# Attention begun behind four of the eight key tiles, the other four projected between its first steps

## The chip, the core and the metric

The kernel runs on one core of a Trainium2 chip. Its engines work side by side, each through its own stream of instructions in order: TensorE (PE) for matmuls, with its weight loads shown as a lane of their own (PEld), VectorE (DVE), ScalarE (ACT), GpSimd (POOL) and SyncE (SP), which here issues the loads of weights. They are ordered among each other by semaphores alone. The metric is the time of one execution on the device in microseconds (us); less is better.

## What is computed

A trunk of two layers over 512 tokens of width 1024. Layer 0 is a recurrent mixer and an MLP; layer 1 is latent attention and an MLP. The change is in the attention of layer 1, eight heads, whose part of the reference is:

```python
q = (rmsnorm(c_q, q_norm) @ w_uq).reshape(B, T, MLA_HEADS, MLA_NOPE + MLA_ROPE)
kv = (rmsnorm(c_kv, kv_norm) @ w_ukv).reshape(B, T, MLA_HEADS, MLA_NOPE + MLA_V)
q_nope, q_rope = q[..., :MLA_NOPE], q[..., MLA_NOPE:]
k_nope, v = kv[..., :MLA_NOPE], kv[..., MLA_NOPE:]
q_rope = rope(q_rope, cos[:, :, None, :], sin[:, :, None, :])
k_rope = rope(k_rope, cos, sin)
# per block of 128 queries, with a block-causal mask over chunks of 64:
s = (einsum('bqhd,bkhd->bhqk', qn, k_nope) + einsum('bqhd,bkd->bhqk', qr, k_rope)) * scale
p = softmax(where(key_chunk <= q_chunk, s, -inf))
o = einsum('bhqk,bkhv->bqhv', p, v)
```

## The kernel before

**Split precision.** Every large product is made of three matmuls (`mm3`, line 1459): a value x is held as a rounded high part and the rest as a low part. So each result that feeds another product is read out of PSUM twice: ACT writes the high part (`key_high`, `query_high`, `rope_high`, `split_high` for weights), DVE subtracts and writes the low part (`key_low`, `query_low`, `rope_low`, `split_low`), and both count up semaphores (kt_high and kt_ready for keys, qn_high and qn_ready for queries, qr_high and qr_ready for rotated queries, hi_ready and lo_ready for weights).

**Units of weights.** Weights come in units, numbered in the order of their use: here ("mv", 0), ("mv", 1), ("qr", 0), ("qn", 0), ("mk", 0), ("mk", 1), then ("qr", a), ("qn", a) for a = 1 to 3, then the output projection. A unit is loaded into one of two stages; SP issues unit u only when unit u - 2 has been split by ACT and by DVE (`stage_free`, line 537 and on). It is then split into one of four slots. `pump(u)` on ACT and on DVE splits unit u + 4 into the slot of unit u; on ACT it first waits until the last tile that uses unit u is done (`tile_of_unit`).

**Tiles and two banks.** A projection is a tile of [128 features x 512 tokens], made by `feature_tile` (line 1469 and on). Tiles are numbered in the order of `add_tile`, tile n goes to bank n % 2, and `wait_bank` (line 455) makes PE wait, ahead of tile n, until tile n - 2 has been read: for a key tile "read" is kt_ready (its low part is written), for ("qn", ...) it is qn_ready, for ("qr", a) it is rot_read (DVE's `rotate(a)` is through). A key tile ("mk", g, j) of head 4g + j has 6 matmuls of 512 columns, a tile of ("qr", a) or ("qn", a, hh) has 9. ("qr", a) holds the rotary part of two heads: DVE multiplies it by cosine and sine (`rotate`), POOL issues four DMAs that swap its halves, DVE adds (`rotated`), ACT and DVE write high and low (`rope_high`, `rope_low`).

**Order around the change.** PE projects ("qr", 0), ("qn", 0, 0), ("qn", 0, 1) and all eight key tiles. Then comes a loop of steps j = 0 to 33, j = 4 h + qb for head h and block of queries qb. In step j PE makes scores(j) (two matmuls of k_rope, three of k_nope, one of the mask, all of width (qb + 1) x 128), then a tile where one is due: ("qr", a) in step 0 of a group of eight, ("qn", a, 0) in step 3, ("qn", a, 1) in step 5, for a = 1 to 3; then transposes(j - 2) of the probabilities; and in each step of j % 4 == 2, from 6 on, values(j // 4 - 1), the product of head j // 4 - 1 with its values. DVE in step j: the row maximum of scores(j) (wait on s_done), the scaling of the probabilities of j - 1, then its share of the projections (`rotate`, `pump`, `rotated`, `query_low`, `rope_low`). ACT in step j: the exponential of j (wait on nmax_ready), the copy of the transposed probabilities of j - 2 (pt_ready; the fourth copy of a head releases its values), then its share of the projections. Each engine takes all this strictly in the order written. scores(0) waits for all eight keys (kt_ready 8) and for the first rotated query (qr_ready 1).

## Time and profile before

| what | us |
|---|---|
| median of the runs | 1265.15 |
| lowest and highest of the three runs | 1263.35 and 1397.88 |
| the profiled execution | 1267.64 |
| its span, first to last instruction | 1265.8 |
| PE busy in the span | 1210.7 (96%) |
| DVE, ACT busy | 663.2, 533.0 |

The profile is of one execution. Its times count from the span's start. The attention steps of layer 1 lie between 768.9 and 853.4 us, and the key tiles stand right ahead of them. A busy PE is not PE at its full clock: the granted clock is given apart, as a share of full speed (1.00 is 2.4 GHz).

### The profile page before, as it was taken

The page shows a single profiled execution, that of the slowest core. Times are in us where ns is not written, and L with a number is a line of the kernel's source. Part 1 is how long each engine was busy: PE and PEld are TensorE (multiplying, and loading weights), DVE is VectorE, ACT ScalarE, POOL GpSimd, SP SyncE. Part 2 cuts the span into 40 slices and gives each one's busy share as a digit, 9 for nine tenths or more (in the row PEclk, how much of TensorE's full clock was granted, in tenths as well). Part 3 has the DMA queues.
Part 4 walks back from the last instruction along what each step waited for, and adds up shares of the span by engine and source line. Part 5 has one row for each costly group of instructions (what it writes and reads, how often), then busy time and mean ns, then how long its engine had stood idle before and what let it go on. Part 6 is the DMA issues. An engine that isn't in the chain of part 4 may idle for free.

```text
span 1265.8 us, 16242 instructions
## 1 busy us (share of the span) xinstructions
PE 1210.7 (96%) x5995; PEld 999.5 (79%) x5995; DVE 663.2 (52%) x1028; ACT 533.0 (42%) x1049; POOL 112.4 (9%) x126
## 2 busy tenths in 40 slices
PE   7899999968999999999999999989999999999997
PEld 5677788857888888888888777767888888888886
DVE  4566877754664443443447257762644443443444
ACT  4554455533642332332535665552642332332332
POOL 2331213200190000000000000100000000000000
PEclk9999999989999999999999899999999999999999
DMA  3322112113322223322222131201332322222221
GB/s 121 109 75 67 51 50 64 54 50 133 124 101 98 86 100 100 99 99 91 93 99 76 56 93 45 84 17 50 106 108 90 97 100 100 96 98 87 99 83 67
DMA packets 87444, 108.23 MB, mean 85 GB/s; under 512 B 9138, under 2 KB 48147, under 8 KB 87380
## 3 DMA queue, kind: packets, MB, share of 16 engines
q1 hardware_dynamic: 85684, 101.85, 25.0%
q0 software_dynamic: 1696, 5.51, 1.3%
q8 instruction: 42, 0.69, 0.2%
q14 instruction: 22, 0.18, 0.0%
HBM read 104.20 MB, written 2.10 MB: 84 GB/s over the span
## 4 chain that ended last, share of the span: by engine, by line
PE 83%; DVE 7%; ACT 6%; issue 2%; DMA 1%; POOL 0%; DVEq 0%; SPq 0%; ACTq 0%
PE bank L1460 25%; PE bank L1461 24%; PE bank L1462 24%; PE pp L1600 1%; PE po L1867 1%; PE pp L1503 1%; PE pp L1461 1%; PE pp L1460 1%; PE pp L1462 1%; ACT w_hi L486 1%; ACT w_hi L484 1%; PE pp L1848 1%; PE po L1611 1%; DVE xl L1122 0%; PE po L1614 0%
## 5 line engine op out<-in xcount | busy, mean ns | idle before, releaser
L1460 PE MATMUL bank<-h_lo,w_hi 128*128 128x512 f32 (+4 forms) x572 | 218.3, 382 | 8.7 <-DVE h_lo L1065 4.2
L1462 PE MATMUL bank<-h_hi,w_hi 128*128 128x512 f32 (+4 forms) x572 | 215.5, 377 | 0.0
L1461 PE MATMUL bank<-h_hi,w_lo 128*128 128x512 f32 (+4 forms) x572 | 215.3, 376 | 0.0
L1460 PE MATMUL bank<-wx,a_hi 128*128 128x512 f32 x320 | 126.6, 396 | 5.4 <-DVE wx L494 5.4
L1460 PEld LDWEIGHTS bank<-h_lo,w_hi 128*128 128x128 f32 (+1 forms) x572 | 106.7, 186 | 31.1 <-issue 5.2
L1288 DVE TENSOR_TENSOR tmp<-sq,bank 128x512 f32<-128x512 f32 x64 | 44.0, 688 | 156.1 <-ACT sq L896 156.1
L1461 PE MATMUL bank<-wx,a_lo 128*128 128x512 f32 x320 | 125.3, 392 | 0.0
L1462 PE MATMUL bank<-wx,a_hi 128*128 128x512 f32 x320 | 125.3, 391 | 0.0
L896 ACT ACTIVATE sq<-bank 128x512 f32<-128x512 f32 x64 | 38.3, 598 | 204.3 <-PE bank L1462 204.3
L1462 PEld LDWEIGHTS bank<-h_hi,w_hi 128*128 128x128 f32 (+1 forms) x572 | 106.8, 187 | 19.8
L1461 PEld LDWEIGHTS bank<-h_hi,w_lo 128*128 128x128 f32 (+1 forms) x572 | 106.8, 187 | 18.2
L1460 PE MATMUL bank<-w_lo,a_hi 128*128 128x512 f32 x304 | 119.7, 394 | 0.9 <-ACT y L972 0.9
L1461 PE MATMUL bank<-w_hi,a_lo 128*128 128x512 f32 x304 | 118.7, 391 | 0.0
L1462 PE MATMUL bank<-w_hi,a_hi 128*128 128x512 f32 x304 | 118.6, 390 | 0.0
L486 ACT ACTIVATE w_hi<-stage,vec 128x512 fp32r<-128x512 f32 (+2 forms) x104 | 62.6, 656 | 103.7 <-PE bank L1462 100.5
L1460 PE MATMUL bank<-h_lo,wx 128*128 128x512 f32 x256 | 99.6, 389 | 0.0
L1461 PE MATMUL bank<-h_hi,wx 128*128 128x512 f32 x256 | 99.6, 389 | 0.0
L1462 PE MATMUL bank<-h_hi,wx 128*128 128x512 f32 x256 | 99.6, 389 | 0.0
L494 DVE TENSOR_TENSOR w_lo<-stage,w_hi 128x1024 fp32r<-128x1024 f32 (+1 forms) x69 | 86.8, 1258 | 21.3 <-ACT w_hi L484 15.7
L1296 DVE TENSOR_TENSOR y<-y,bank 128x512 f32<-128x512 f32 x48 | 33.0, 687 | 108.0 <-PE bank L1462 108.0
L496 DVE SCALAR_TENSOR_TENSOR w_lo<-stage,vec,w_hi 128x512 fp32r<-128x512 f32 (+2 forms) x104 | 65.1, 670 | 28.6 <-ACT w_hi L486 28.5
L1460 PEld LDWEIGHTS bank<-wx,a_hi 128*128 128x128 f32 x320 | 60.5, 189 | 20.0 <-DVE wx L494 7.8
(312 smaller groups left out, 2063.3 us busy)
## 6 DMA issues: line engine op xcount, KB each, us to landing
stage<-in_mlp_w SPq DMA_DIRECT2D x128, 512.0 KB, 3.5
stage<-in_ev_w_in SPq DMA_DIRECT2D x28, 512.0 KB, 3.7
stage<-in_ev_w_out SPq DMA_DIRECT2D x8, 512.0 KB, 3.6
stage<-in_od_w_out SPq DMA_DIRECT2D x8, 512.0 KB, 3.6
stage<-in_od_w_in SPq DMA_DIRECT2D x10, 256.0 KB, 3.0
x_tok<-in_x SPq DMA_DIRECT2D x4, 512.0 KB, 5.3
gbc<-in_norm_gains POOLq DMA_DIRECT2D x4, 512.0 KB, 4.3
xr<-in_x POOLq DMA_DIRECT2D x1, 2048.0 KB, 9.0
```

What stands on the lines that cost most here:

```text
L484: ins = nc.scalar.copy(hi[:, c], stage[:, u % STAGE, c])
L486: ins = nc.scalar.activation(hi[:, c], stage[:, u % STAGE, c], ACT.Copy, scale=vec[:, g:g + 1])
L494: ins = nc.vector.tensor_tensor(lo[:, c], stage[:, u % STAGE, c], hi[:, c].bitcast(F32), ALU.subtract)
L496: ins = nc.vector.scalar_tensor_tensor(out=lo[:, c], in0=stage[:, u % STAGE, c], scalar=vec[:, g:g + 1], in1=hi[:, c].bitcast(F32), op0=AL ...
L896: nc.scalar.activation(sq[:, m % 2, :], bank[n % 2][:, :], ACT.Relu).then_inc(relu_ready[layer], 1)
L1288: nc.vector.tensor_tensor(tmp[:, m % 2, :], sq[:, m % 2, :], bank[n % 2][:, :], ALU.mult).then_inc(hid_f32[layer], 1)
L1296: nc.vector.tensor_tensor(y[:, ys, :], y[:, ys, :], bank[n % 2][:, :], ALU.add).then_inc(y_ready[j], 1)
L1460: nc.tensor.matmul(dst, wh, xl_, start=first, stop=False)
L1461: nc.tensor.matmul(dst, wl, xh, start=False, stop=False)
L1462: return nc.tensor.matmul(dst, wh, xh, start=False, stop=last)
L1503: ins = nc.tensor.transpose(turn_bank(t, q)[:, a, :], xr[:, 2 * t + q, a * P:(a + 1) * P], ident[:, :])
L1600: ins = nc.tensor.matmul(dst[o], k_, q_, start=True, stop=True)
```

## The change

Ahead of the steps only the keys of heads 0 to 3 are projected. The key tiles of heads 4, 5, 6 and 7 follow on PE in steps 1, 2, 4 and 7, between the tiles of the queries; tiles are numbered in the new order. scores at the start of a head waits for the key of that head (at least four keys). ACT reads the new tiles in steps 2, 3, 5 and 8 (KEY_HIGH), DVE in steps 3, 4, 7 and 9 (KEY_LOW). rotated(0) on DVE moves from behind key 3 to behind key 1, and rope_high(0) and rope_low(0) come behind key 3. The pumps of ("mk", 1), ("qr", 1) and ("qn", 1) stood behind the last key, in step 1 (ACT) or 2 (DVE), and in step 6 or 7; all three now stand in step 8 on ACT and in step 9 on DVE. No instruction is added or taken away but for the semaphore waits.

```diff
--- before.py
+++ after.py
@@ -212,18 +212,16 @@
         for g in range(2):
             u = add_unit((what, g), [((KV_RANK_T, 4 * P), None, k, w_kv[k, :, 4 * g:4 * g + 4, c0:c0 + P])
                                      for k in range(KV_RANK_T)], [V_KVN, V_KVN + 1])
-            for j in range(4):
-                add_tile((what, g, j), u)
+            if what == "mv":
+                for j in range(4):
+                    add_tile((what, g, j), u)
 
     def add_q(a):
         c = 2 * a * (NOPE + ROPE)
         u = add_unit(("qr", a), [((Q_RANK_T, P), hh * ROPE, (hh + 1) * ROPE,
                                   rows(w_q, c + hh * 192 + NOPE, c + (hh + 1) * 192)) for hh in range(2)], q_gains)
-        add_tile(("qr", a), u)
         u = add_unit(("qn", a), [((Q_RANK_T, 2 * P), hh * P, (hh + 1) * P, rows(w_q, c + hh * 192, c + hh * 192 + NOPE))
                                  for hh in range(2)], q_gains)
-        add_tile(("qn", a, 0), u)
-        add_tile(("qn", a, 1), u)
 
     w_kv, w_q = w, mla_w_uq[0]
     q_gains = [V_QN + k for k in range(Q_RANK_T)]
@@ -232,6 +230,17 @@
     add_kv("mk", 0)
     for a in range(1, MLA_HEADS // 2):
         add_q(a)
+    FIRST_KEYS = 4
+    SIDE_TILES = {}
+    for a in range(1, MLA_HEADS // 2):
+        for step, tile in ((0, ("qr", a)), (3, ("qn", a, 0)), (5, ("qn", a, 1))):
+            SIDE_TILES[8 * (a - 1) + step] = tile
+    for step, h in ((1, 4), (2, 5), (4, 6), (7, 7)):
+        SIDE_TILES[step] = ("mk", h // 4, h % 4)
+    for tile in [("qr", 0), ("qn", 0, 0), ("qn", 0, 1)] + [("mk", 0, h) for h in range(FIRST_KEYS)]:
+        add_tile(tile, unit_no[tile[:2]])
+    for step in sorted(SIDE_TILES):
+        add_tile(SIDE_TILES[step], unit_no[SIDE_TILES[step][:2]])
     add_out("oo", od_w_out[0], range(4))
     add_mlp(1)
     n_units = len(units)
@@ -1006,17 +1015,15 @@
                 act.wait_ge(pv_done, h + 1)
                 nc.scalar.copy(a_hi[:, h, :], po[:, :]).then_inc(att_high, 1)
 
+            KEY_HIGH = {2: 4, 3: 5, 5: 6, 8: 7}
             pump(unit_no[("qr", 0)])
             query_high(0)
             query_high(1)
             pump(unit_no[("qn", 0)])
-            for h in range(MLA_HEADS):
+            for h in range(FIRST_KEYS):
                 key_high(h)
-                if h == 4:
-                    rope_high(0)
-                if h == 5:
-                    pump(unit_no[("mk", 0)])
-            pump(unit_no[("mk", 1)])
+            rope_high(0)
+            pump(unit_no[("mk", 0)])
 
             for j in range(4 * MLA_HEADS + 2):
                 if j < 4 * MLA_HEADS:
@@ -1034,8 +1041,10 @@
                     nc.scalar.copy(turned_probs(h)[:, 0:qb + 1, qb * P:(qb + 1) * P],
                                    t_bank[i % 2][:, 0:qb + 1, :]).then_inc(pt_ready, 1)
                 a, step = j // 8 + 1, j % 8
+                if j in KEY_HIGH:
+                    key_high(KEY_HIGH[j])
                 if a < MLA_HEADS // 2:
-                    if step == 1:
+                    if step == 1 and a > 1:
                         pump(unit_no[("qr", a)])
                     elif step == 4:
                         query_high(2 * a)
@@ -1043,7 +1052,12 @@
                         rope_high(a)
                     elif step == 6:
                         query_high(2 * a + 1)
-                        pump(unit_no[("qn", a)])
+                        if a > 1:
+                            pump(unit_no[("qn", a)])
+                if j == 8:
+                    pump(unit_no[("mk", 1)])
+                    pump(unit_no[("qr", 1)])
+                    pump(unit_no[("qn", 1)])
                 if j >= 7 and j % 4 == 3:
                     att_out(j // 4 - 1)
             att_out(MLA_HEADS - 1)
@@ -1407,14 +1421,13 @@
             query_low(0)
             query_low(1)
             pump(unit_no[("qn", 0)])
-            for h in range(MLA_HEADS):
+            KEY_LOW = {3: 4, 4: 5, 7: 6, 9: 7}
+            for h in range(FIRST_KEYS):
                 key_low(h)
-                if h == 3:
+                if h == 1:
                     rotated(0)
-                if h == 5:
-                    pump(unit_no[("mk", 0)])
-                    rope_low(0)
-            pump(unit_no[("mk", 1)])
+            pump(unit_no[("mk", 0)])
+            rope_low(0)
 
             for j in range(4 * MLA_HEADS + 2):
                 if j < 4 * MLA_HEADS:
@@ -1432,10 +1445,16 @@
                     nc.vector.tensor_scalar(prob[:, i % 3, 0:width], prob[:, i % 3, 0:width], stat[:, 2, i:i + 1], None,
                                             ALU.mult).then_inc(prob_ready, 1)
                 a, step = j // 8 + 1, j % 8
+                if j in KEY_LOW:
+                    key_low(KEY_LOW[j])
+                if j == 9:
+                    pump(unit_no[("mk", 1)])
+                    pump(unit_no[("qr", 1)])
+                    pump(unit_no[("qn", 1)])
                 if a < MLA_HEADS // 2:
                     if step == 1:
                         rotate(a)
-                    elif step == 2:
+                    elif step == 2 and a > 1:
                         pump(unit_no[("qr", a)])
                     elif step == 4:
                         rotated(a)
@@ -1445,7 +1464,8 @@
                         rope_low(a)
                     elif step == 7:
                         query_low(2 * a + 1)
-                        pump(unit_no[("qn", a)])
+                        if a > 1:
+                            pump(unit_no[("qn", a)])
                 if j >= 8 and j % 4 == 0:
                     att_out(j // 4 - 2)
             att_out(MLA_HEADS - 1)
@@ -1825,9 +1845,12 @@
             project_qr(0)
             project_qn(0)
             project_qn(1)
-            for h in range(MLA_HEADS):
+            def project_k(h):
                 g, j = divmod(h, 4)
                 feature_tile(unit_no[("mk", g)], tile_no[("mk", g, j)], a_hi, a_lo, kt=KV_RANK_T, cols=T, c0=j * P)
+
+            for h in range(FIRST_KEYS):
+                project_k(h)
 
             def scores(j):
                 h, qb = divmod(j, 4)
@@ -1840,8 +1863,8 @@
                 if qb == 0:
                     pe.wait_ge(qr_ready, 2 * a + hh + 1)
                     pe.wait_ge(qn_ready, h + 1)
-                if j == 0:
-                    pe.wait_ge(kt_ready, MLA_HEADS)
+                if qb == 0:
+                    pe.wait_ge(kt_ready, max(h + 1, FIRST_KEYS))
                 q_hi, q_lo = query(h)
                 k_hi, k_lo = key(h)
                 for part in range(2):
@@ -1874,12 +1897,14 @@
             for j in range(4 * MLA_HEADS + 2):
                 if j < 4 * MLA_HEADS:
                     scores(j)
-                a, step = j // 8 + 1, j % 8
-                if a < MLA_HEADS // 2:
-                    if step == 0:
+                if j in SIDE_TILES:
+                    what, a, *hh = SIDE_TILES[j]
+                    if what == "qr":
                         project_qr(a)
-                    elif step in (3, 5):
-                        project_qn(2 * a + step // 4)
+                    elif what == "qn":
+                        project_qn(2 * a + hh[0])
+                    else:
+                        project_k(4 * a + hh[0])
                 if 2 <= j:
                     transposes(j - 2)
                 if j >= 6 and j % 4 == 2:
```

## Rows read from the trace of the kernel before

**Rows 1.** Page, engine table: busy us, share of the span, instructions

```profile
PE 1210.7 (96%) x5995; PEld 999.5 (79%) x5995; DVE 663.2 (52%) x1028; ACT 533.0 (42%) x1049; POOL 112.4 (9%) x126
```

**Rows 2.** Busy us in stretches: length, PE, PEld, DVE, ACT, POOL, granted clock, DMA share, GB/s

```profile
759.80:768.92 9.12, 6.39 (x25) 4.24 (x25) 6.48 (x13) 6.17 (x13) 0.00 (x0) 1.00 0.10 23
768.92:788.00 19.08, 18.90 (x96) 15.66 (x97) 12.58 (x38) 10.51 (x29) 1.97 (x4) 0.91 0.22 63
788.00:809.33 21.33, 20.46 (x114) 16.60 (x113) 16.82 (x45) 13.39 (x33) 1.97 (x4) 1.00 0.20 62
830.59:853.38 22.79, 17.32 (x94) 13.90 (x93) 14.41 (x43) 11.08 (x31) 0.00 (x0) 0.93 0.07 23
```

**Rows 3.** Timeline, PE around the last key tiles: start, us, engine, line, operation, [idle before]

```profile
759.54 0.39 PE L1462 MATMUL bank<-a_hi,w_hi 128*128 128x512 f32 x1
...
764.97 0.47 PE L1460 MATMUL bank<-a_lo,w_hi 128*128 128x512 f32 x1
...
766.20 0.40 PE L1462 MATMUL bank<-a_hi,w_hi 128*128 128x512 f32 x1
...
768.92 0.41 PE L1848 MATMUL pp<-kr,q_rope 128*128 128x128 f32 x2 [2.33 <-DVE k_last L1364]
...
769.62 0.50 PE L1460 MATMUL bank<-h_lo,w_hi 128*128 128x512 f32 x1
...
772.90 0.58 PE L1462 MATMUL bank<-h_hi,w_hi 128*128 128x512 f32 x1
...
776.68 0.45 PE L1460 MATMUL bank<-h_lo,w_hi 128*128 128x512 f32 x1
...
778.81 0.38 PE L1859 MATMUL misc<-ident,prob 128*128 128x128 f32 x2
```

**Rows 4.** Timeline, ACT and DVE from key 3 to the last key

```profile
759.97 0.60 ACT L997 ACTIVATE a_hi<-bank 128x512 fp32r<-128x512 f32 x1 [0.76 <-PE bank L1462]
...
762.23 1.25 ACT L1003 CAST q_rope<-q_sum_f 64x512 fp32r<-64x512 f32 x2
...
764.13 0.99 ACT L486 ACTIVATE w_hi<-stage,vec 128x128 fp32r<-128x128 f32 x3
...
765.15 0.88 DVE L496 SCALAR_TENSOR_TENSOR w_lo<-stage,vec,w_hi 128x128 fp32r<-128x128 f32 x3 [0.32 <-ACT w_hi L486]
766.05 1.40 DVE L1393 TENSOR_TENSOR q_rope<-q_sum_f,q_rope 64x512 fp32r<-64x512 f32 x2
...
768.10 0.68 DVE L1364 TENSOR_TENSOR k_last<-bank,k_last 128x512 fp32r<-128x512 f32 x1
```

**Rows 5.** Timeline, scores of steps 7 and 4 and DVE's instruction behind their statistics

```profile
786.56 0.71 PE L1848 MATMUL pp<-kr,q_rope 128*128 128x512 f32 x2
...
789.44 0.69 DVE L1370 TENSOR_TENSOR h_lo<-bank,h_hi 128x512 fp32r<-128x512 f32 x1
...
778.95 0.42 PE L1848 MATMUL pp<-kr,q_rope 128*128 128x128 f32 x2
...
780.90 0.69 DVE L1387 TENSOR_TENSOR q_sum_f<-q_sum_f,rinv 128x512 f32<-128x512 f32 x1
```

**Rows 6.** Timeline, steps 8 to 10, a split of ("qn", 2) and a load

```profile
788.00 0.42 PE L1848 MATMUL pp<-kr,q_rope 128*128 128x128 f32 x2
...
791.09 0.48 PE L1848 MATMUL pp<-kr,q_rope 128*128 128x256 f32 x2
...
793.57 0.56 ACT L1025 ACTIVATE prob<-pp,stat,tok 128x256 f32<-128x256 f32 x1 [0.85 <-DVE stat L1425]
...
794.75 2.42 PE L1867 MATMUL po<-y,v_tok 128*128 128x512 f32 x8 [0.44 <-ACT y L1034]
...
767.13 1.29 ACT L486 ACTIVATE w_hi<-stage,vec 128x256 fp32r<-128x256 f32 x3
...
770.04 0.90 SPq L551 DMA_DIRECT2D stage<-in_mla_w_uq  x2
```

**Rows 7.** DMA issues from 769.9 to 774 us: KB each, us to landing

```profile
stage<-in_mla_w_uq SPq DMA_DIRECT2D x2, 192.0 KB, 2.7
```

## What the change should do to the time

> **What bounds the kernel now.** I read the page first, for its engine table: TensorE (PE) is busy for 96% of the span, so what an edit is worth is what it does to PE's idle time and to PE's clock [rows 1]. Then the busy time of stretches, cut at the attention's own marks [rows 2]: the last four key tiles and the wait behind them (759.80 to 768.92), steps 0 to 7 (768.92 to 788.00), steps 8 to 15, and the last eight steps. The reader is to see that PE is idle for 2.7 of the 9.12 us of the first stretch, for 0.2 of the 19.08 us of the second, and for 5.5 us of the last, which has no projections in it. So steps 0 to 7, where the new tiles go, hold no idle time for them to fill; the idle time lies ahead of them, and at the far end, which the change does not touch.
>
> Then the timeline of PE around the key tiles [rows 3]. The fourth key tile's last matmul starts at 759.54, the eighth tile's six run from 764.97 to 766.20, and the first scores start only at 768.92: a wait of 2.33 us for the low part of the last key. The granted clock then falls: the nine matmuls of the tile ("qr", 1) go from 769.62 to 773.33 (3.70 us, 0.43 each, the 1.2 GHz level), where the nine of ("qn", 1, 0) take 2.13 us (776.68 to 778.81, the 2.4 GHz level). That is 1.57 us lost to the clock.
>
> **Part 1, the start.** Removed ahead of the first scores: key tiles 4 to 7. What is last there afterwards? PE ends the fourth key tile at 759.8 as before, but scores(0) also needs q_rope of head 0, and its chain has to be redone [rows 4]. ACT takes key_high(3) at 759.97 and is free at 760.47. rotated(0) is moved ahead of the third key, where DVE is idle, so rope_high(0) follows at once: 1.25 us, to 761.75. Then ACT splits the unit of pump(("mk", 0)), 1.0 us, to 762.75. DVE has that pump ahead of rope_low(0): 0.9 us, to 763.65, then the first half of rope_low, 0.7 us, to 764.35; with the 0.14 us from DVE's end to PE's start that the old wait shows (k_last's end at 768.78), scores(0) starts at 764.5. PE is idle from 759.9 to 764.5, 4.6 us where it was idle 2.3. scores(0) is earlier by 768.92 - 764.5 = **4.4 us**, though 9.15 us of tiles and waits were taken from in front of it: the wait has changed its owner. The weights of this pump were loaded long before, so nothing is to wait for there.
>
> **Part 2, the tiles in the steps.** A key tile costs PE 6 matmuls: 764.97 to 766.20, plus 0.23 for the last, about 1.43 us [rows 3]. Four are 5.7 us. As steps 0 to 7 have no idle time [rows 2], all of it is added: **+5.7 us**. The clock's 1.57 us is in the 19.08 us of these steps already; the longer idle time ahead of them leaves no reason for less, so I keep it.
>
> **Part 3, the bank of two tiles ago.** A projection waits in PE's stream until the tile two numbers earlier has been read out of its bank. Before, those were tiles read long ago. With the new order the tile of step 3 waits for key 4, that of step 4 for key 5, that of step 5 for the query of step 3, and that of step 7 for key 6, and the DVE instruction that reads them stands in the same step (KEY_LOW 3, 4, 7; query_low in 5), behind that step's row maximum, which waits for that step's scores. PE has just issued the scores and stands behind them. How long, the trace shows with the same shapes: in step 7 of before the scores start at 786.56 and query_low, at the place of the new key_low, starts at 789.44 and lasts 0.69: 3.6 us after the scores' start, with a little for the signal; the four-block scores take PE 1.30, so the wait is 2.3 us. In step 4 the scores start at 778.95 and the instruction behind the statistics at 780.90; one of 0.69 us there ends 2.7 us after the scores' start, and they take PE 0.7: 2.0 us [rows 5]. Steps 3 and 7 have the first form, steps 4 and 5 the second (5 rather less: 1.9). Step 2 waits for rotate(1), which ends just when PE arrives, so 0 to 0.1. Sum 2.3 + 2.0 + 2.0 + 2.3 = **+8.6 us**. Behind each waiting tile stand the transposes of that step and all later scores; ACT and DVE then wait for them, so nothing is made up. A gain is excluded, zero would need PE to take later matmuls first.
> The page TensorE: Matmul & The Clock Gate of the Trainium skill (The mechanism) says that only weight loads are pulled ahead, and that matmuls start and end in program order. By that rule the four waits count in full, as the sum has them; by the opposite the sum would be 8.6 us smaller. The trace has no matmul out of order in any stretch that I read.
>
> **Part 4, three pumps in one place.** pump(("mk", 1)), pump(("qr", 1)) and pump(("qn", 1)) move to step 8 on ACT and step 9 on DVE. They split the units ("qn", 2), ("qr", 3), ("qn", 3). There are two stages; the first two units lie in them, but the load of ("qn", 3) is issued by SP only when ("qn", 2) has been split by DVE too. Before, that was at 770.04, ahead of the steps; now ACT stands in step 8 until it lands. Queued behind on ACT: the exponential of step 9 and the copy that turned probabilities of head 1 need, and for that copy waits values(1) on PE in step 10. From the start of scores(8) [rows 6]: 3.1 us to scores(9) (788.00 to 791.09), about 1.05 for the copy and key_high(7) (0.5 each, as key_high in [rows 4]), 1.3 for the high split (767.13 has the same), 1.4 for DVE's low split with its start, 2.7 from issue to landing ([rows 7]; the issue at 770.04 is this very load), 1.3 for the high split of ("qn", 3), 1.2 from the start of the exponential over the copy to values(1) (793.57 to 794.75), 0.4 for the starts between: 12.5 us. Before, values(1) came 6.75 us after scores(8) (794.75). **+5.75 us**, with PE idle for some 7 us. DVE meanwhile stands in the same pump and comes back to its statistics before PE has finished values(1) and the next scores; the following load (od_w_out) is issued 1 us behind and lands in the same wait; rotate(2) is late by the same wait, but so is rotated(2) in step 12, which needs POOL's four DMAs behind it.
> **Part 5, the clock.** An idle time of 7 us is longer than the 2.3 us behind which the clock fell before [rows 3]. I take one tile's loss for it, **+1.6 us**, with 0 and twice that as bounds. Steps 0 to 7 would be idle for 8.6 of about 33 us, 26%; the last eight steps of before are idle for 24% of theirs and show a granted clock of 0.93, that is 7% of 22.8 us twice over, 3.2 us, at the 1.2 GHz level [rows 2], which costs at most half, 1.6 us. I take the same for steps 3 to 7, **+1.6 us**, with 0 and 3.2 as bounds.
>
> **Sum.** -4.4 + 5.7 + 8.6 + 5.75 + 1.6 + 1.6 = +18.85 us. The profiled execution took 1267.64 us (span 1265.8 and 1.8 around it) and would take 1286.5. The runs shown have a median of 1265.15, 2.5 us lower, so the forecast for the median is 1284.0 us. No DMA, split or matmul is added or removed in number; from step 11 on the order is that of before and I expect no difference.
>
> **Rivals.** (a) The bank waits are hidden, because PE passes them or because DVE is ahead: +18.85 - 8.6 - 1.6 = +8.65, 1273.8 us. Against it: DVE cannot read a row maximum before the scores are there. Chance 0.08. (b) The load of ("qn", 3) is hidden: without its 5.75 us and the 1.6 of clock behind it, +11.5, 1276.7 us. For it speaks only that the wait is in program order on ACT and not on PE; against it, the load cannot be issued earlier. Chance 0.10. (c) The other side: the early start decides. If q_rope of head 0 is ready by 761.4 and PE then finds its banks free, scores(0) starts at 761.5, 7.4 us earlier, the wait of 2.33 us and the 1.57 us of lower clock are gone: -7.4 + 5.7 - 1.6 = -3.3, 1261.9 us. It decides only if the waits of parts 3 and 4 together stay below 3.3 us, where I count over 14. Chance 0.04. (d) The clock falls behind each of the four waits of part 3, not in one stretch only: 4 times 1.57 in place of 1.6 is +23.5, 1288.7 us. For it: each of them is about as long as the 2.33 us behind which it fell [rows 3]; against it: the last eight steps, idle nearly as much, lost it for 3 us only [rows 2]. Chance 0.10. My forecast: 0.68.
>
> **How the numbers follow.** The likeliest case gives 1284.0. Its own bounds: with both terms of part 5 at 0, +15.65 (1280.8); with both at 3.2, +22.05 (1287.2). To hold it eight times in ten the range takes in (a) and (b) below and (d) above, with 1 us for signals and queues: 1274 to 1290 us. 2% of this kernel, about what a measurement can tell from no change, is 25 us: only (d) with something on top reaches it, 0.04; no case reaches 2% faster, 0.01 is left for what I did not see; 0.95 within.
>
> **What would show it.** Scores(0) about 4.7 us behind the fourth key tile, released by DVE's q_rope and not by a key. PE waiting about 2.3, 2.0, 1.9 and 2.3 us ahead of the projections of steps 3, 4, 5 and 7, released by DVE's low parts. Steps 0 to 7 lasting about 33 us in place of 19.1. The load of ("qn", 3) issued behind DVE's split of step 9, and values(1) released by ACT about 12.5 us after scores(8) start. Wrong would be a start of scores(0) near 761.5, PE without waits in steps 3 to 7, or a change later than step 16.

## The result, and the profile after

| what | before | after |
|---|---|---|
| median of the runs, us | 1265.79 | 1292.87 (lowest 1287.7, highest 1294.13) |
| ratio to before | 1 | 1.0213, 95% interval 1.0175 to 1.025 |
| the profiled execution, us | 1267.64 | 1292.99 |
| its span, us | 1265.8 | 1291.3 |

The kernel is slower by 2.1%, 27 us in the medians. The forecast was 1284.0 us with a range up to 1290, so the sign was right, the size was 9 us short and the range ended 3 us too low. (The interval of the ratio, on 1265.8 us, is 1287.9 to 1297.4; it holds 2% inside, so the runs do not tell on which side of 2% the change lies.) One execution of before took 1397.88 us, in a second, slower state of the chip, and the ratio leaves it out.

The engine table of the page of after, against [rows 1]:

```profile
span 1291.3 us, 16249 instructions
PE 1221.0 (95%) x5995; PEld 1007.0 (78%) x5995; DVE 662.9 (51%) x1028; ACT 533.5 (41%) x1049; POOL 111.8 (9%) x126
```

Read it before any timeline. PE executes the same 5995 matmuls and is busy 10.3 us longer, so its matmuls themselves last longer; that this is its clock is what the granted clock of the stretches below says and what runs 5 and 6 test. Its idle time grew from 55.1 us (1265.8 - 1210.7) to 70.3 us, by 15.2. So 15 us are waits and 10 us are longer matmuls. The terms of the forecast amount to 16.2 us of idle time (4.6 for 2.73 us ahead of scores(0), 8.6, 5.75) and 3.2 us of clock: the waits were foreseen, the clock was not.

Busy us in stretches of after, cut at the same marks as [rows 2]: from the end of the fourth key tile to scores(0), steps 0 to 7, scores(8) to values(1), values(1) to scores(16), and on to the end of the attention. Columns as in [rows 2].

```profile
760.07:764.74 4.67, 0.05 (x1) 0.03 (x1) 2.48 (x7) 2.70 (x6) 0.00 (x0) 1.00 0.00 0
764.74:804.41 39.67, 31.35 (x121) 25.33 (x121) 15.41 (x41) 11.14 (x28) 1.97 (x4) 0.76 0.05 13
804.41:817.59 13.18, 6.23 (x38) 5.60 (x36) 6.26 (x19) 6.83 (x19) 0.00 (x0) 0.76 0.23 70
817.59:834.82 17.23, 17.23 (x76) 13.20 (x77) 11.40 (x29) 9.66 (x22) 1.97 (x4) 0.84 0.25 77
834.82:878.87 44.05, 37.74 (x204) 30.29 (x203) 31.04 (x86) 24.40 (x63) 1.97 (x4) 0.96 0.14 42
```

And the last three of these stretches in before, which [rows 2] did not cut this way:

```profile
788.00:794.75 6.75, 5.88 (x38) 4.92 (x36) 6.48 (x19) 3.74 (x12) 0.00 (x0) 1.00 0.22 78
794.75:809.33 14.58, 14.57 (x76) 11.69 (x77) 10.34 (x27) 9.65 (x22) 1.97 (x4) 1.00 0.19 55
809.33:853.38 44.05, 37.75 (x205) 30.50 (x204) 31.16 (x86) 24.45 (x63) 1.97 (x4) 0.96 0.13 42
```

The last stretch is 44.05 us in both, so everything happens ahead of scores(16). All lengths below are counted "from key 3", that is from the start of the fourth key tile's last matmul (759.54 in before, 759.73 in after), since a profile can reach this place some 5 us earlier or later than another for reasons upstream (755.34 in run 10, 760.64 in run 4). From key 3 to scores(16): 49.79 us before, 75.09 us after, **+25.3 us**.

PE in after, the rows that carry a wait in steps 0 to 10 (start, us, engine, line, operation, [idle before it, and what released it]), against [rows 3]:

```profile
764.74 0.42 PE L1871 MATMUL pp<-kr,q_rope 128*128 128x128 f32 x2 [4.62 <-issue]
...
777.60 0.47 PE L1480 MATMUL bank<-h_lo,w_hi 128*128 128x512 f32 x1 [2.25 <-DVE a_lo L1378]
...
778.97 0.63 PE L1482 MATMUL bank<-h_hi,w_hi 128*128 128x512 f32 x1
...
784.27 0.47 PE L1480 MATMUL bank<-a_lo,w_hi 128*128 128x512 f32 x1 [1.92 <-DVE a_lo L1378]
...
789.77 0.77 PE L1480 MATMUL bank<-h_lo,w_hi 128*128 128x512 f32 x1 [1.85 <-DVE h_lo L1384]
...
793.33 0.63 PE L1482 MATMUL bank<-h_hi,w_hi 128*128 128x512 f32 x1
...
801.94 0.47 PE L1480 MATMUL bank<-a_lo,w_hi 128*128 128x512 f32 x1 [2.25 <-DVE h_lo L1378]
...
817.59 4.63 PE L1890 MATMUL po<-y,v_tok 128*128 128x512 f32 x8 [6.95 <-ACT y L1041]
```

Four waits of 2.25, 1.92, 1.85 and 2.25 us stand ahead of the projections of steps 3, 4, 5 and 7, each released by DVE's low part of the tile two numbers earlier; the prediction had 2.3, 2.0, 1.9 and 2.3 ([rows 5] was enough to get them). scores(0) starts at 764.74, forecast 764.5; the 4.62 us ahead of it carry "issue" for a releaser, but DVE's rope_low starts at 763.85, its two halves take 1.40 us together, and the first ends just there; run 6 names it as the releaser. What [rows 3] could not show is the matmuls' own length: 0.63 us for 0.39 us, and starts 0.43 us apart for 0.23 (the 1.2 GHz level for the 2.4 GHz one), from the middle of the tile of step 3, and in the whole tile of step 5 (789.77 to 793.75, 3.98 us; at full clock 2.13).

The chain of the long wait, on DVE, SP and ACT of after, against [rows 6]:

```profile
810.76 2.05 DVE L505 SCALAR_TENSOR_TENSOR w_lo<-stage,vec,w_hi 128x256 fp32r<-128x256 f32 x6
...
812.10 0.90 SPq L560 DMA_DIRECT2D stage<-in_mla_w_uq  x2
...
815.22 1.30 ACT L495 ACTIVATE w_hi<-stage,vec 128x256 fp32r<-128x256 f32 x3 [3.66 <-DMA stage<-in_mla_w_uq]
...
816.43 0.55 ACT L1032 ACTIVATE prob<-pp,stat,tok 128x256 f32<-128x256 f32 x1
```

DVE's low split frees the stage at about 812.1, SP issues the load, ACT's split starts on it at 815.22 (3.1 us behind the issue; the forecast put the 2.7 of [rows 7] there, which is the median of the two transfers' own times and is 2.5 in after), ACT splits for 1.3 us and only then gets to the exponential of step 9. values(1) starts 13.18 us after scores(8), forecast 12.5, before 6.75.

### The profile page after: what moved, and what is told of

It is laid out like the page before. It is cut to its first block, busy times and chain, and to the rows that moved or that the text cites. A ratio compares the mean times of both kernels' runs of the same rounds, so it can differ in the third digit from the quotient of the medians.

```text
span 1291.3 us, 16249 instructions
## 1 busy us (share of the span) xinstructions
PE 1221.0 (95%) x5995; PEld 1007.0 (78%) x5995; DVE 662.9 (51%) x1028; ACT 533.5 (41%) x1049; POOL 111.8 (9%) x126
## 4 chain that ended last, share of the span: by engine, by line
PE 83%; DVE 7%; ACT 6%; issue 2%; DMA 1%; POOL 0%; DVEq 0%; SPq 0%; ACTq 0%
PE bank L1480 25%; PE bank L1482 24%; PE bank L1481 24%; PE po L1890 2%; PE pp L1620 1%; PE pp L1523 1%; PE pp L1480 1%; PE pp L1481 1%; PE pp L1482 1%; PE pp L1871 1%; ACT w_hi L495 1%; ACT w_hi L493 1%; PE po L1631 1%; DVE stat L1436 1%; DVE xl L1136 0%
## 5 line engine op out<-in xcount | busy, mean ns | idle before, releaser
L1480 PEld LDWEIGHTS bank<-wx,a_hi 128*128 128x128 f32 x320 | 60.4, 189 | 19.6 <-DVE wx L503 7.5
```

Source lines behind the costliest of these rows:

```text
L1480: nc.tensor.matmul(dst, wh, xl_, start=first, stop=False)
```

## The experiments

Each kernel is after or before with the edit shown. Two theories stand against each other at first. The one on record: the time lies in two waits that can be taken away one by one, the reads behind the row maximum and the load behind the third pump, and the clock adds a few us. The rival: the waits matter mostly for the clock that falls behind them, so that a kernel with the same waits and a busy PE would lose far less. All ratios are to before, run on the same chip, with 95% intervals.

**1. e1_pump: the second and third pump four steps later.** After, with the pumps of ("qn", 1) in step 12; to keep the order of units, the next one, ("qr", 2), goes there too.

```diff
# on ACT, and the same on DVE (there from step 9)
                 if j == 8:
                     pump(unit_no[("mk", 1)])
                     pump(unit_no[("qr", 1)])
+                if j == 12:
                     pump(unit_no[("qn", 1)])
+                    pump(unit_no[("qr", 2)])
-                    if step == 1 and a > 1:
+                    if step == 1 and a > 2:
```

> The changed kernel with one edit: pump(("qn", 1)), and with it pump(("qr", 2)) behind it, moved to step 12 on ACT and DVE. Theory 1 (the load of ("qn", 3) is waited for in step 8 and its idle time also lowers the clock): PE's wait of 6.95 us ahead of values(1) goes to below 1 us, values(1) starts about 7 us after scores(8) in place of 13.2, the stretch behind it takes 14.6 us in place of 17.2; about 9 us less than the changed kernel, about +16.5 us (1.013) against before. Rival (the wait is hidden or turns up again at the next pump of step 12): no more than 2 us less, +23 to +25 us. Steps 0 to 7 stay at 39.7 us in both.

Measured: 1286.05 us, ratio 1.0161 [1.0132, 1.0189], +20.6. Windows of steps 0 to 7, of scores(8) to values(1), and of values(1) to scores(16), and two waits of PE:

```profile
761.68:799.29 37.61, 29.29 (x121) 23.82 (x121) 15.41 (x41) 11.13 (x28) 1.97 (x4) 0.81 0.06 13
799.29:806.77 7.48, 5.50 (x38) 4.85 (x36) 5.04 (x16) 5.47 (x15) 0.00 (x0) 1.00 0.00 0
806.77:829.05 22.28, 18.46 (x76) 13.26 (x77) 12.54 (x32) 10.79 (x25) 1.97 (x4) 0.85 0.32 101
```

```profile
806.77 4.12 PE L1894 MATMUL po<-y,v_tok 128*128 128x512 f32 x8 [1.99 <-ACT y L1041]
...
822.97 0.33 PE L1886 MATMUL pp<-ident,prob 128*128 128x128 f32 x1 [3.38 <-DVE prob L1447]
```

The load wait is gone from scores(8) to values(1) (13.18 to 7.48 us), as expected. But two pumps in one place are still one too many: in step 12 DVE stands 2.08 us for ACT's splits, PE then waits 3.38 us for DVE's probabilities, and the last stretch grows from 17.23 to 22.28 us. The 5.7 us that were won were paid back to all but 0.65 us. So the expectation missed by 4 us, and the trace puts this down to the two pumps in step 12; run 2, which separates them, tests that.

**2. e10_pumps_apart: one pump a step.** After, with the pumps in steps 8, 9 and 10 on ACT and 9, 10 and 11 on DVE, and ("qr", 2) in 12 and 13.

```diff
                 if j == 8:
                     pump(unit_no[("mk", 1)])
+                if j == 9:
                     pump(unit_no[("qr", 1)])
+                if j == 10:
                     pump(unit_no[("qn", 1)])
+                if j == 12:
+                    pump(unit_no[("qr", 2)])
```

> The changed kernel with the three pumps in steps of their own (ACT 8, 9, 10, DVE 9, 10, 11, that of ("qr", 2) in 12 and 13), everything else as changed. In e1_pump, with two pumps in step 12, values(1) still waited 1.99 us and the transposes of step 14 waited 3.38 us for DVE. Theory (the size of these was the crowding of pumps in one step): both go below 1 us, values(1) about 6.5 us after scores(8), 14.6 us from there to scores(16): 9 us less than the changed kernel, about +17.5 us against before. Rival (a late load is waited for wherever its pump stands): about e1_pump's +20.6 us.

Measured: 1281.75 us, ratio 1.0131 [1.0108, 1.0153], +16.9. The same three stretches:

```profile
762.29:801.00 38.71, 30.41 (x120) 24.38 (x121) 15.39 (x41) 11.13 (x28) 1.96 (x4) 0.81 0.05 12
801.00:807.91 6.91, 5.79 (x37) 5.20 (x36) 4.18 (x13) 4.66 (x13) 0.00 (x0) 0.95 0.00 0
807.91:822.50 14.59, 14.59 (x77) 11.71 (x77) 13.31 (x35) 11.52 (x28) 1.96 (x4) 1.00 0.50 154
```

Now part 4 of the change is undone alone: 6.91 and 14.59 us, where before has 6.75 and 14.58. The stretches from scores(8) to scores(16) give back 8.9 us of the 9.1 they had lost, 6.3 of it the wait and 2.6 the clock behind it. It is the same three pumps and the same loads, and PE no longer waits for them (1.12 us of idle time are left ahead of values(1), 0.44 in before).

**3. e4_pumps_alone: part 4 alone, on before.** Before, with the three pumps in step 8 (ACT) and 9 (DVE) and nothing else.

```diff
-            pump(unit_no[("mk", 1)])
...
+                if j == 8:
+                    pump(unit_no[("mk", 1)])
+                    pump(unit_no[("qr", 1)])
+                    pump(unit_no[("qn", 1)])
```

> The kernel before with one edit: the pumps of ("mk", 1), ("qr", 1) and ("qn", 1) in step 8 on ACT and step 9 on DVE, as the changed kernel has them; all eight key tiles still ahead of the steps. Theory 1: values(1) starts about 13 us after scores(8) in place of 6.75, with a lower clock behind it, less what the pumps no longer cost ahead of steps 0 to 7 (about 1 us at scores(0), as DVE's split stands behind k_last there): +8 to +9 us against before (1.007). Rival (the wait needs the late key tiles too, since key_high(7) and key_low(7) stand ahead of the pumps): below +3 us.

Measured: 1273.35 us, ratio 1.0059 [1.004, 1.0078], +7.9. Stretches as above, and the wait:

```profile
767.72:786.59 18.87, 18.69 (x97) 15.71 (x97) 10.84 (x32) 8.47 (x23) 1.96 (x4) 0.91 0.07 15
786.59:799.35 12.76, 5.45 (x38) 4.85 (x37) 7.66 (x23) 7.06 (x20) 0.00 (x0) 0.84 0.25 72
799.35:816.95 17.60, 17.60 (x76) 13.43 (x77) 11.40 (x29) 9.68 (x22) 1.96 (x4) 0.82 0.23 75
```

```profile
799.35 3.35 PE L1875 MATMUL po<-y,v_tok 128*128 128x512 f32 x4 [7.31 <-ACT y L1033]
```

The other way round, the same sum: +6.0 for the wait, +3.0 for the clock behind it, 8.8 us from key 3 to scores(16). Part 4 costs 8.8 us in this trace and 9.9 between after and run 2 (7.5 and 10.4 by the ratios), whatever stands ahead of it; it and the rest of the change add, to about 1 us in the traces and 3 us by the ratios.

**4. e2_reads: the bank waits taken away.** After, with the readers of the late tiles moved ahead of their step's row maximum on DVE, and ahead of the copy of the probabilities on ACT. The waits go because the reader comes earlier in DVE's order; no semaphore is dropped.

```diff
# on DVE, at the top of a step, ahead of the row maximum
+                if j in (3, 4, 7):
+                    key_low(KEY_LOW[j])
+                if j == 5:
+                    query_low(2)
# on ACT, behind the exponential, ahead of the copy of the turned probabilities
+                if j in KEY_HIGH:
+                    key_high(KEY_HIGH[j])
+                if j == 4:
+                    query_high(2)
```

> The changed kernel with one edit: key_low(4), key_low(5), query_low(2) and key_low(6) on DVE ahead of the row maximum of steps 3, 4, 5 and 7 and not behind it, and on ACT the high parts of the same tiles ahead of the copy of the probabilities. Theory 2 (PE waits because the reader of the bank stands behind the same step's scores, and these waits lower the clock of steps 0 to 7): the four waits of 2.25, 1.92, 1.85 and 2.25 us fall below 0.5 us each, the granted clock of steps 0 to 7 rises from 0.76 to about 0.9, the steps take about 25 us in place of 39.7: 14 us less than the changed kernel, about +11.5 us (1.009) against before. Rival A (the 4.6 us idle ahead of scores(0) lower the clock, not the waits): the waits fall but the clock stays, 8 us less, +17.5 us. Rival B (DVE and ACT are the bound of these steps): waits come back elsewhere and nothing is gained.

Measured: 1279.1 us, ratio 1.0111 [1.0073, 1.0149], +13.7, 13.8 us below after. Steps 0 to 7, and scores(8) to values(1):

```profile
765.65:791.78 26.13, 25.88 (x121) 21.04 (x121) 15.32 (x41) 10.85 (x28) 1.96 (x4) 0.90 0.08 19
791.78:804.28 12.50, 5.51 (x38) 4.86 (x36) 6.63 (x20) 6.95 (x20) 0.00 (x0) 0.90 0.24 73
```

All four waits are gone: PE is idle for 0.25 us of the eight steps instead of 8.32. But the stretch shrank by 13.5 us, not by 8.1, and the granted clock rose from 0.76 to 0.90. The waits thus cost what they last and, in these two profiles, two thirds as much again. This is the row that decides against the sizing of part 5.

**5. e3_fill: the same waits, PE kept busy.** After, with 9, 8, 7 and 9 matmuls added in the four waits, into a bank of scores that is free there. Nothing reads their results and nothing is left out, so this kernel does 33 matmuls more than after.

```diff
+            def filler(b, count, done):
+                if done > 0:
+                    pe.wait_ge(prob_exp, done)
+                for _ in range(count):
+                    nc.tensor.matmul(s_bank[b][:, :], kr[:, 0, 0:P], kr[:, 0, :], start=True, stop=True)
+            FILL_STEPS = {3: 9, 4: 8, 5: 7, 7: 9}
...
+                if j in FILL_STEPS:
+                    filler((j + 1) % 3, FILL_STEPS[j], j - 1)
```

> The changed kernel with filler matmuls that nothing reads (128x512, into the score bank that comes next): 9, 8, 7 and 9 of them ahead of the bank waits of steps 3, 4, 5 and 7, about as long as the waits. No wait is removed. Theory 2 (idle PE in these waits lowers the clock, worth 5 to 6 us beyond the waits): the clock of steps 0 to 7 rises from 0.76 to 0.9 and they take about 34 us in place of 39.7, though PE has 33 matmuls more; about 5.5 us less than the changed kernel, about +20 us against before. Rival A (the clock falls for another reason, such as the 4.6 us idle ahead of scores(0)): the clock stays and the kernel is as slow as the changed one or slower by the 33 matmuls at the lower level, 0 to +7 us on top.

Measured: 1285.11 us, ratio 1.0155 [1.0127, 1.0183], +19.7, 7.8 us below after. Steps 0 to 7, and the fillers of step 3 with the tile behind them:

```profile
764.05:797.45 33.40, 32.90 (x153) 26.13 (x154) 15.41 (x41) 11.15 (x28) 1.96 (x4) 0.95 0.07 15
```

```profile
774.50 2.29 PE L1899 MATMUL pp<-kr 128*128 128x512 f32 x9
776.91 0.47 PE L1480 MATMUL bank<-h_lo,w_hi 128*128 128x512 f32 x1
...
778.15 0.39 PE L1482 MATMUL bank<-h_hi,w_hi 128*128 128x512 f32 x1
```

The tile of step 3 starts no earlier behind its scores than in after (776.91 - 774.44 = 2.47 us behind the mask's matmul, in after 777.60 - 775.13 = 2.47), yet its matmuls take 0.39 us. The wait is there in full and the clock is not lost: the stretch is 33.40 us where it was 39.67. A kernel that computes more is faster, and what changed is what PE did while it waited.

**6. e6_fill_all: every wait filled.** As 5, with 19 matmuls more ahead of scores(0) and 28 ahead of values(1).

```diff
-            filler(2, 0, 0)
+            filler(2, 19, 0)
...
                 if j == 10:
-                    filler(2, 0, 9)
+                    filler(2, 28, 9)
```

> The changed kernel with filler matmuls in all its long waits: as e3_fill, and 19 ahead of scores(0) (4.6 us idle) and 28 ahead of values(1) (7 us idle). No wait is removed. My theory: with PE busy through them, the clock stays at its upper level, so the 1.6 us at scores(0) and the 2.6 us behind values(1) are saved on top of e3_fill: about 4 to 5 us less than e3_fill, about +15.5 us against before. If the clock had another reason than PE's idle time, it is e3_fill's +19.7 us or more.

Measured: 1277.44 us, ratio 1.0084 [1.0063, 1.0105], +11.3. Steps 0 to 7, scores(8) to values(1), values(1) to scores(16):

```profile
763.33:795.20 31.87, 31.37 (x154) 24.86 (x154) 15.56 (x41) 11.13 (x28) 1.96 (x4) 1.00 0.07 15
795.20:807.68 12.48, 11.86 (x66) 9.95 (x65) 6.26 (x19) 6.83 (x19) 0.00 (x0) 1.00 0.24 75
807.68:822.26 14.58, 14.58 (x77) 11.69 (x77) 11.33 (x29) 9.64 (x22) 1.96 (x4) 1.00 0.29 90
```

The clock is 1.00 throughout. The row of scores(0) now names its releaser:

```profile
763.33 0.44 PE L1871 MATMUL pp<-kr,q_rope 128*128 128x128 f32 x2 [0.17 <-DVE q_rope L1407]
```

The waits stand where they stood (12.48 us to values(1) against 13.18), and steps 0 to 7 are 7.8 us shorter than in after, the last stretch 2.65. The whole price of the clock in after is so measured at once: from key 3 to scores(16) 75.09 against 63.79 us, 11.3 us; the medians differ by 15.4. Against run 5 the expectation was 4 to 5 us less: the traces give 4.3 (68.13 - 63.79), the ratios 9.0. So the +11.3 for an expected +15.5 is no sign of a dearer clock in this stretch; the profiled execution, 1281.36 us, is the slowest of the four, the others took 1274.8 to 1277.9, and no trace shows where they are shorter.

**7. e8_before_fill: is the clock a part of before too?** Before, with 10 matmuls in the 2.33 us ahead of scores(0) [rows 3], results read by nothing.

```diff
             pe.wait_ge(rope_ready, 1)
+            for _ in range(10):
+                nc.tensor.matmul(s_bank[2][:, :], kr[:, 0, 0:P], kr[:, 0, :], start=True, stop=True)
             for j in range(4 * MLA_HEADS + 2):
```

> The kernel before with 10 filler matmuls (128x512) that nothing reads ahead of scores(0), where PE is idle for 2.33 us. Theory (idle PE lowers the clock, 1.57 us lost in the tile of step 0): the tile takes 2.1 us in place of 3.7, 1.5 us faster than before (0.9988), though no wait is gone and PE does more. Rival (the clock of that moment does not follow the idle time): same as before or slower.

Measured: 1264.76 us, ratio 0.9993 [0.9979, 1.0007]. Not to be told from before in time, and the 1.5 us that were expected (0.9988) lie in the interval just as no difference does. In the trace the effect is there:

```profile
766.87:784.65 17.78, 17.56 (x96) 14.55 (x97) 12.65 (x38) 10.29 (x29) 1.96 (x4) 1.00 0.24 68
```

```profile
764.38 2.45 PE L1875 MATMUL pp<-kr 128*128 128x512 f32 x10
```

Steps 0 to 7 take 17.78 us at clock 1.00 where [rows 2] have 19.08 at 0.91: 1.3 us, the price of one idle time of 2.33 us in these two profiles. It gives the yardstick as well: the work of these steps is 17.56 us of PE at full clock, and in after's form 23.30 us (run 8).

**8. e5_both: both causes taken away.** After, with the reads of run 4 and the pumps of run 2; and rope_low(0) ahead of the pump of ("mk", 0) on DVE, so that the start of scores(0) does not wait for a split.

```diff
# on DVE, in place of pump first, rope_low second
+            rope_low(0)
             pump(unit_no[("mk", 0)])
-            rope_low(0)
```

> The changed kernel with the readers moved forward as in e2_reads, the three pumps spread (ACT steps 8, 9, 10, DVE 9, 10, 11, and that of ("qr", 2) in 12 and 13), and rope_low(0) ahead of the pump of ("mk", 0) on DVE. My theory (waits at the banks, one wait for a load, and the clock that falls behind each is all that the change costs beyond its 5.7 us of moved tiles): no wait over 1 us between scores(0) and step 16, scores(0) 0.9 us earlier than in the changed kernel, steps 0 to 7 26 us, values(1) 7 us after scores(8); about 25 us less than the changed kernel, 0 to +3 us against before. Rival (ACT and DVE have too much to do in these steps, so that waits turn up elsewhere): +7 us or more.

Measured: 1264.33 us, ratio 0.9981 [0.9963, 0.9999], -2.4 by the ratio, better than the 0 to +3 us expected. The wait of scores(0), and two stretches:

```profile
762.97 0.41 PE L1885 MATMUL pp<-kr,q_rope 128*128 128x128 f32 x2 [2.29 <-DVE a_lo L1384]
```

```profile
762.97:786.54 23.57, 23.30 (x120) 19.00 (x121) 16.08 (x44) 11.32 (x30) 1.96 (x4) 1.00 0.09 21
786.54:792.67 6.13, 5.50 (x38) 4.86 (x37) 4.07 (x13) 4.82 (x15) 0.00 (x0) 1.00 0.00 0
```

All that the change lost is gone, with four key tiles ahead and four between the steps as in after. What is left of it is its gain, and that is small: scores(0) comes 2.68 us after key 3 instead of 9.38 (6.7 us earlier), the tiles cost 5.7 us again in the steps, 1.3 us of clock come back there (18.90 busy for 17.56 in before), and scores(8) to scores(16) are 0.6 us shorter. scores(0) is now released by key 3 itself, with an idle time of 2.29 us, as long as the one before [rows 3]; behind this one the clock stayed at 1.00, while behind the 2.33 us of run 3, as in before, it fell (steps 0 to 7 at 0.91).

**9. e7_six: six keys ahead.** Since the idle time ahead of scores(0) only moves, from behind key 7 to behind key 3, two more tiles should fill it. FIRST_KEYS = 6, keys 6 and 7 in steps 1 and 2, the reads as in run 4, rope_high(0) and rope_low(0) behind key 3, and scores waiting for its own head's key alone; the pumps left nearer to their old places (steps 3, 5 and 6).

```diff
-    FIRST_KEYS = 4
+    FIRST_KEYS = 6
-    for step, h in ((1, 4), (2, 5), (4, 6), (7, 7)):
+    for step, h in ((1, 6), (2, 7)):
...
-                    pe.wait_ge(kt_ready, max(h + 1, FIRST_KEYS))
+                    pe.wait_ge(kt_ready, h + 1)
```

> Six keys ahead of the steps, the other two in steps 1 and 2; scores at the start of a head wait for that head's key alone; rope_high(0) and rope_low(0) behind key 3, the readers of the late keys ahead of the row maximum of steps 3 and 4, pumps in steps 3, 5, 6 (ACT) and 4, 5, 7 (DVE). My theory: the chain of q_rope of head 0 (about 4 us behind key 3) is covered by two key tiles (2.9 us), PE's idle time ahead of scores(0) goes below 1 us, the clock stays up (1.6 us), and no projection waits for a reader: 3 to 5 us faster than before (0.997). Rival (any key tile in the steps costs more than the idle time it fills ahead of them): slower than before by 1 us or more.

Measured: 1264.13 us, ratio 0.9989 [0.9976, 1.0002]: not to be told from before, where 3 to 5 us less were expected. Steps 0 to 7 and scores(8) to scores(16), a wait of DVE and one of PE behind it:

```profile
760.68:783.28 22.60, 20.88 (x110) 16.79 (x108) 15.81 (x45) 12.91 (x35) 1.96 (x4) 1.00 0.19 52
783.28:805.08 21.80, 20.46 (x111) 16.61 (x112) 17.33 (x46) 14.76 (x36) 1.96 (x4) 1.00 0.24 71
```

```profile
779.81 0.88 DVE L505 SCALAR_TENSOR_TENSOR w_lo<-stage,vec,w_hi 128x128 fp32r<-128x128 f32 x3 [2.97 <-ACT w_hi L495]
...
782.52 0.44 PE L1884 MATMUL misc<-ident,prob 128*128 128x128 f32 x2 [1.20 <-DVE prob L1450]
```

The start is what it should be (scores(0) 3.33 us behind key 3, two tiles between them), but DVE waits 2.97 us in a pump for ACT's split, PE behind it for 1.20 us in step 7 and in three more places, up to values(1), for 1.66 together. PE is idle for 1.72 us of steps 0 to 7. Run 10, where the pumps stand elsewhere, has 20.58 us for these 22.60 and 20.51 for these 21.80, so 3.3 of the 6.05 us won at the start are lost to pumps in the wrong steps; the two tiles in the steps take 2.9 more.

**10. e9_six_spread: six keys, and the pumps apart.** As 9, with pump(("qr", 1)) in step 4 on ACT, ("qn", 1) in 10 and 11, ("qr", 2) in 12 and 13; the lines shown are against after.

```diff
-                if j == 8:
+                if j == 3:
                     pump(unit_no[("mk", 1)])
+                if j == 4:
                     pump(unit_no[("qr", 1)])
+                if j == 10:
                     pump(unit_no[("qn", 1)])
+                if j == 12:
+                    pump(unit_no[("qr", 2)])
```

> e7_six with two pumps moved: that of ("qr", 1) one step earlier on ACT (4 in place of 5, where DVE had waited 2.97 us for it), that of ("qn", 1) to steps 10 and 11 and of ("qr", 2) to 12 and 13, as in e5_both. Theory (e7_six kept the clock at 1.00 in steps 0 to 7 but gave back 2.4 us to waits for DVE in steps 5 to 10): those waits of 1.2, 0.33, 0.89 and 0.44 us shrink to below 1 us together, values(1) 6.2 us after scores(8): 2 to 3 us faster than e7_six, 4 to 6 us faster than before (0.996). Rival (the waits belong to the moved keys' readers and not to the pumps): no faster than e7_six.

Measured: 1260.21 us, ratio 0.9965 [0.9952, 0.9978]: by the ratios 4.4 us faster than before and 31 us faster than after. Scores(0), steps 0 to 7, and scores(8) to values(1):

```profile
758.50 0.39 PE L1494 MATMUL bank<-a_hi,w_hi 128*128 128x512 f32 x1
758.72 0.33 PE L1883 MATMUL pp<-kr,q_rope 128*128 128x128 f32 x2
```

```profile
758.72:779.30 20.58, 20.38 (x109) 16.76 (x108) 16.29 (x45) 12.99 (x35) 1.96 (x4) 1.00 0.24 68
779.30:785.22 5.92, 5.50 (x39) 4.86 (x37) 5.39 (x16) 3.74 (x10) 0.00 (x0) 1.00 0.00 0
```

scores(0) follows the sixth key's last matmul with nothing between. The idle time of [rows 3] is filled, not moved, no wait has come in its place, and the clock is 1.00. This is a gain of the change's idea, and it is 0.35%; 0.8 us of the 5.3 in the trace lie in scores(8) to scores(16), where only pumps were moved, and no run has those moves without the tiles.

**All of them side by side.** From the traces: us from key 3 to scores(0); steps 0 to 7; scores(8) to scores(16); the sum of the three less before's 49.79. Beside it the ratio to before, less 1, times 1265.4 us.

| kernel | key 3 to scores(0) | steps 0 to 7 | scores(8) to scores(16) | trace | runs |
|---|---|---|---|---|---|
| before | 9.38 | 19.08 | 21.33 | 0 | 0 |
| after | 5.01 | 39.67 | 30.41 | +25.3 | +27.0 |
| e1_pump | 5.01 | 37.61 | 29.76 | +22.6 | +20.4 |
| e10_pumps_apart | 5.02 | 38.71 | 21.50 | +15.4 | +16.6 |
| e4_pumps_alone | 9.40 | 18.87 | 30.36 | +8.8 | +7.5 |
| e2_reads | 5.01 | 26.13 | 29.18 | +10.5 | +14.0 |
| e3_fill | 5.02 | 33.40 | 29.71 | +18.3 | +19.6 |
| e6_fill_all | 4.86 | 31.87 | 27.06 | +14.0 | +10.6 |
| e8_before_fill | 9.36 | 17.78 | 21.32 | -1.3 | -0.9 |
| e5_both | 2.68 | 23.57 | 20.71 | -2.8 | -2.4 |
| e7_six | 3.33 | 22.60 | 21.80 | -2.1 | -1.4 |
| e9_six_spread | 3.38 | 20.58 | 20.51 | -5.3 | -4.4 |

The two last columns agree to 3.5 us, so this stretch explains each time to that much; the rest is within what a place upstream moves from profile to profile. The two parts of the change add: after less e10 is 9.9 us in the trace, e4 alone 8.8.

## Why the prediction was right in kind and wrong in size

The step that failed is part 5, the clock: +1.6 us on record for steps 3 to 7, where the trace shows +6.7. The sum on record was +18.85 us, the trace shows +25.3. By its steps:

- **Part 1, the start:** forecast -4.4, measured -4.37 (5.01 us from key 3 to scores(0), 9.38 before). Right, with its mechanism: run 8, which takes the pump from in front of rope_low(0), moves the release from the rope to the key.
- **Part 2, the tiles:** forecast +5.7, measured +5.74: PE's busy time of the eight steps at full clock is 23.30 us with the tiles (run 8) and 17.56 without (run 7).
- **Part 3, the banks:** forecast +8.6, measured +8.14 (8.32 us idle in after's steps, 0.18 in before's). The four waits came out within 0.1 us each (the sum took 2.0 for the third, which its own text has as 1.9), and run 4 removes them by moving the reader. Rival (a), a hidden bank wait, is out.
- **Part 4, the load:** forecast +5.75, measured +6.43. Of the 0.7 us missed, step 8 itself is longer by 0.7 (scores(9) starts 3.82 us behind scores(8), not 3.1, at a granted clock of 0.80), from the issue of the load to ACT's split it is 3.12 us and not 2.7, and the 0.4 us set aside for starts were not needed. Runs 2 and 3 show the part by itself from both sides. Rival (b) is out.
- **Part 5, the clock: the step that failed.** In steps 3 to 7 it had +1.6 (bounds 0 and 3.2). After is busy for 31.35 us with 23.30 us of work, so 8.05 us are clock; before has 18.90 for 17.56, 1.34 us. Measured: **+6.7 us**, 5.1 more than forecast and twice the upper bound. Behind the long wait it had +1.6, measured +2.65 (17.23 for 14.58 us).

These add up: -4.37 + 5.74 + 8.14 + 6.43 + 6.71 + 2.65 = +25.30. Of the 6.45 us missed, 5.1 lie in the clock of the steps, 1.05 in the clock behind the wait, 0.7 in part 4, and the banks give 0.5 back. (The sign given for steps 0 to 7, about 33 us, left out the forecast's own clock: with it they come to 35.0, and they took 39.67.) The record gave 0.95 to the change staying within 2% and 0.04 to more; the measured 2.1%, with 2% inside its interval, settles neither. The miss of the median is 2.5 us larger because the prediction took before's profiled time down by 2.5 us to the median, while after's profiled execution is at its median.

Why part 5 was too small can be read in its own words: it took the share of idle time (26% of the steps) and looked up a stretch with a like share, the last eight steps of before, with clock 0.93 [rows 2]. But a share does not say how the idle time is cut. There it comes in short pieces, six waits that the timeline marks, the longest 1.58 us; here as four of about 2 us each, at 775, 782, 788 and 800 us, after 4.6 us ahead of the first. That this difference decides the price is an argument, no run tests it. The nearer row was in hand: one idle time of 2.33 us, clock 0.91 over the steps [rows 2, 3]. It is what rival (d) was built on, 4 x 1.57 = 6.3 us, and the steps measured 6.7. Rival (d), at 0.10, was the mechanism: in after there are matmuls at the lower level behind each of the four waits, and step 0 pays for the idle time ahead of it as before did (4.41 us from scores(0) to scores(1), 4.40 in before), as part 2 had kept it. That its size fits so well is partly luck, since the same four waits cost less in two other kernels (below). Its term took the place of part 5's, and with it the sum would have been 1288.7; with the larger term behind the long wait, 1289.7. The remaining 3 us are part 4's 0.7 and the 2.5 above.

That the clock, and not some slowness of operands or banks, made these matmuls long is shown by runs 5 and 6: same waits, same order, same operands, 80 matmuls more, and 11.3 us less in the trace. The Trainium skill, page TensorE: Matmul & The Clock Gate (A second HAM failure mode: psum-queue depth-cycling), describes that frequent short idle times between groups of matmuls, as banks are cycled, can make the clock swing between its two levels. This trace agrees: matmuls of 512 columns go from 0.39 to 0.63 us and back several times in 40 us, and the prediction did not weigh that section.

**What stays open.** The price of the same waits is not one number. With the same four waits the steps lose 8.05 us in after, 7.1 in run 2 (30.41 - 23.30) and 6.0 in run 1 (29.29 - 23.30), though the three kernels do the same there; and an idle time of 2.3 us ahead of scores(0) cost 1.34 us in before and nothing in run 8. Step 0 can be taken apart from the rest, since from scores(0) to scores(1) it lasts 2.81 us in run 8, at clock 1.00. In after and in run 4:

```profile
764.74:769.15 4.41, 4.41 (x15) 3.73 (x16) 1.01 (x3) 0.55 (x2) 0.00 (x0) 0.61 0.21 48
765.65:770.91 5.26, 5.26 (x16) 4.39 (x16) 1.01 (x3) 0.55 (x2) 0.00 (x0) 0.50 0.16 37
```

Behind the same 4.62 us of idle time step 0 loses 1.6 us in after and run 5, 2.0 in run 1 and 2.4 in runs 2 and 4; in run 4 that is nearly all of the 2.6 us of clock that are left (25.88 - 23.30). The four waits alone then cost 6.4 us in after, 4.7 in run 2 and 4.0 in run 1. No run here tells what decides it, and one profiled execution of each is too few to give a spread. The whole kernel moves with it: the four executions of after took 1287.7, 1292.74, 1292.99 and 1294.13 us at a mean granted clock of 0.981, 0.977, 0.975 and 0.973. So the size of the miss is itself uncertain by some microseconds, and one of the four lies inside the forecast range; that the clock term was too small is not, as the lowest price of the four waits seen, 4.0 us, is above the bound of 3.2.

## What to carry to other kernels

When a tile is slotted between the steps of a loop, ask first who must have read the bank it goes to, and where that reader stands in its own engine's order: behind this step's scores it makes PE wait for what PE has just done, ahead of them it costs nothing (13.5 us of 39.7 here). Price every idle time of PE that is new and about 2 us long with the clock behind it, one by one and not by the share of idle time: here 4.0 to 6.4 us on top of 8.3 us of waits, in three kernels. And do not put the splits of a two-stage ring in one place without looking which load waits for them: here three pumps in a row turned a hidden load of 3 us into a wait of 7 us, and one pump a step hid it.

## What the runs showed of the hardware

- A PE that waits can be made faster by giving it work that nothing reads. 33 such matmuls in the four waits took steps 0 to 7 from 39.67 to 33.40 us, and 80 in all waits brought the granted clock of the whole stretch to 1.00 and the kernel from ratio 1.0213 to 1.0084. It is a measuring instrument before it is a remedy: it separates what a wait lasts from what it does to the clock. In before it won 1.3 us in the trace and nothing that the runs could tell (0.9993 [0.9979, 1.0007]).
- The clock can fall some matmuls behind the wait. In after the tile of step 3 starts at 777.60, behind 2.25 us of idle time, with matmuls of 0.39 us, and goes over to 0.63 us only from 778.97 on, in the middle of its nine; the tiles of steps 4 and 7 do the like, while the tile of step 5 (789.77) and scores(0) are slow from their first matmul. So the first rows behind a wait do not tell what it costs: the whole tile has to be read.
- At a granted clock of 1.00 the same work is steady to 0.01 us: values(1) to scores(16) took 14.58, 14.59, 14.58, 14.58 and 14.59 us in before and in runs 2, 6, 8 and 10.
